# The long convolutions' filter on four quadrants of TensorE's array instead of two

## What is computed

```python
    h = jnp.sin(freq * (h @ w3 + b3))
    h = (h @ w_proj).reshape(L, HYENA_ORDER, N_DIRECTIONS, HYENA_WIDTH)
    ...
    decay = jnp.exp(-t * jnp.abs(deltas)[None, :])
    return h * decay[:, None, None, :]

def two_sided_spectrum(h):
    ...
    k_full = jnp.concatenate([k_fwd, jnp.zeros_like(k_fwd[:1]), k_bwd[:0:-1]], axis=0)
    return jnp.fft.rfft(k_full, n=2 * L, axis=0)

    for o in range(HYENA_ORDER):
        y = gates[o] * fft_conv(y, k_f[:, o], hyena_d[o])
```

## Time and profile before

| | |
|---|---|
| median of 3 runs | 4593.53 us |
| the profiled execution | 4597.2 us |
| its span (first to last instruction) | 4595.4 us |
| TensorE busy (PE) | 4273.0 us, 93% |
| VectorE busy (DVE) | 2845.9 us, 62% |
| ScalarE busy (ACT) | 1916.2 us, 42% |
| mean granted clock of TensorE | 0.967 of full speed |
| the jobs of the long convolutions | 2220 to 2690 us of the span |

### The profile page before, as it was taken

One profiled execution on the slowest core, in us unless ns is written; L12 is line 12 of the kernel. 1 busy time (PEld: TensorE's weight loads), 2 busy tenths in 40 slices (PEclk: granted clock), 3 DMA queues, 4 the chain that ended last, 5 costly groups with the idle time before them and its releaser, 6 DMA issues.

```text
span 4595.4 us, 62423 instructions
## 1 busy us (share of the span) xinstructions
PE 4273.0 (93%) x24340; PEld 3462.5 (75%) x24372; DVE 2845.9 (62%) x3887; ACT 1916.2 (42%) x3543; POOL 1126.8 (25%) x733
## 2 busy tenths in 40 slices
PE   7999999999899989999899979899999998988689
PEld 4888888889788777788677658677878777766467
DVE  5688888871666532045466667475675673577666
ACT  5111111111566631122566546454564562466453
POOL 2111111110333311011021112453554442233212
PEclk9999999999999999999999989999999999999799
DMA  4111111122544321111589852444434334443663
GB/s 169 51 51 51 51 51 51 55 68 90 190 131 132 120 99 48 55 65 66 203 273 292 281 215 90 124 136 127 142 115 129 118 123 126 124 118 108 193 194 133
DMA packets 606956, 569.59 MB, mean 124 GB/s; under 512 B 59772, under 2 KB 517312, under 8 KB 601674
## 3 DMA queue, kind: packets, MB, share of 16 engines
q1 hardware_dynamic: 557630, 482.52, 33.9%
q10 hardware_dynamic: 49036, 83.09, 4.9%
HBM read 385.61 MB, written 179.90 MB: 123 GB/s over the span
## 4 chain that ended last, share of the span: by engine, by line
PE 74%; DVE 10%; ACT 6%; issue 4%; DMA 4%; SPq 2%; POOL 1%; ACTq 0%; DVEq 0%; POOLq 0%
PE ps L227 10%; PE ps L226 10%; PE ps L228 10%; PE ps L252 3%; PE ps L251 3%; PE ps L253 3%; PE ps L3604 2%; PE ps L3605 2%; PE ps L3606 2%; DVE rec_x L3338 2%; PE ps L3725 2%; PE ps L2488 1%; PE ps L2487 1%; PE ps L2489 1%; PE ps L239 1%
## 5 line engine op out<-in xcount | busy, mean ns | idle before, releaser
L226 PE MATMUL ps<-hh,wsplit 128*128 128x512 f32 x2048 | 819.2, 400 | 8.2 <-DVE hl L1376 4.3
L227 PE MATMUL ps<-hl,wsplit 128*128 128x512 f32 x2048 | 814.1, 397 | 0.0
L228 PE MATMUL ps<-hh,wsplit 128*128 128x512 f32 x2048 | 809.1, 395 | 0.0
L952 DVE SCALAR_TENSOR_TENSOR conv_acc<-conv_in,pcol,conv_acc 128x1024 f32<-128x1024 f32 x480 | 687.9, 1433 | 14.8
L218 POOL TENSOR_TENSOR wsplit<-wraw,wsplit 128x1024 fp32r<-128x1024 f32 x72 | 201.9, 2815 | 1347.1 <-ACT wsplit L213 1347.1
L2822 POOL TENSOR_TENSOR w<-w_raw,w 128x1024 fp32r<-128x1024 f32 x144 | 352.5, 2454 | 647.0 <-ACT w L2816 646.8
L226 PEld LDWEIGHTS ps<-hh,wsplit 128*128 128x128 f32 x2048 | 387.3, 189 | 108.9 <-issue 7.4
L227 PEld LDWEIGHTS ps<-hl,wsplit 128*128 128x128 f32 x2048 | 390.3, 191 | 93.4 <-issue 4.3
L228 PEld LDWEIGHTS ps<-hh,wsplit 128*128 128x128 f32 x2048 | 386.2, 189 | 88.3
L3604 PE MATMUL ps<-h_hi,w 128*128 128x512 f32 x896 | 376.6, 420 | 4.4 <-DVE h_lo L3392 4.4
L3605 PE MATMUL ps<-h_lo,w 128*128 128x512 f32 x896 | 358.7, 400 | 0.0
(11 more groups left out here) (389 smaller groups left out, 9249.3 us busy)
## 6 DMA issues: line engine op xcount, KB each, us to landing
w_raw<-in_w_in SPq DMA_DIRECT2D x144, 512.0 KB, 4.2
wraw<-in_w_in SPq DMA_DIRECT2D x72, 512.0 KB, 3.9
sh<-hy_ak ACTq DMA_DIRECT2D x48, 512.0 KB, 3.8
g_tiles<-b_ost SPq DMA_DIRECT2D x80, 256.0 KB, 3.5
wo_raw<-in_w_out SPq DMA_DIRECT2D x32, 512.0 KB, 5.6
sh<-hy_ad ACTq DMA_DIRECT2D x32, 512.0 KB, 9.5
hy_kt<-sh SPq DMA_DIRECT2D x32, 512.0 KB, 7.1
hy_dd<-sh SPq DMA_DIRECT2D x32, 512.0 KB, 6.7
```

The lines of the kernel that those rows point to most:

```text
L226: e.matmul(p[:, :], wh, c.HH[tb][:, k, :], start=k == 0, stop=False)
L227: e.matmul(p[:, :], wh, c.HL[tb][:, k, :], start=False, stop=False)
L228: t = e.matmul(p[:, :], wl, c.HH[tb][:, k, :], start=False, stop=k == 7)
L952: e.scalar_tensor_tensor(v, a[:, h * 1024 + j:(h + 1) * 1024 + j], c.convw(j, ch), v, ALU.mult, ALU.add) \
```

## The change

`hy_filter` takes two banks at a time, for groups g and g + 1. The even group is made as before. For the odd group the halves are written crosswise: the forward half of `G` goes to the bank's partitions 64 to 127, the backward one to 0 to 63. So four matmuls in a row use the four quadrants. There is one signal for a pair instead of one for a group, and VectorE's product of an odd group waits for the same signal as that of the even one. What stands crosswise is put right by data: the times of the decay are exchanged for the odd groups, and wk uses for them a second matrix, `WK[1]`, which is `WK` with its rows rolled by 64. The constant k_wk is 256 columns wide now, and it takes one more DMA of 64 KB. Some constants lie elsewhere in SBUF.

```diff
-    k["k_wk"] = wk
+    k["k_wk"] = np.concatenate([wk, np.roll(wk, 64, axis=0)], 1)
...
-    k["k_time"] = -np.concatenate([ends[tf.T], ends[tb.T]], 0)
+    times = np.concatenate([ends[tf.T], ends[tb.T]], 0).reshape(128, 4, 2, 4)
+    times[:, :, 1] = np.roll(times[:, :, 1], 64, axis=0)
+    k["k_time"] = -times.reshape(128, 32)
...
+    L.WK = [view("hy_wk", at_wk, 128), view("hy_wk_turned", al(128), 128)]
...
-        for n, (dst, src) in enumerate([(L.WK, A["k_wk"]), (flat(L.WA), A["k_wa"]), (flat(L.WAI), A["k_wai"]), (L.rate, A["k_rate"]), (L.time, A["k_time"])]):
+        for n, (dst, src) in enumerate([(L.WK[0], A["k_wk"][:, 0:128]), (L.WK[1], A["k_wk"][:, 128:256]), (flat(L.WA), A["k_wa"]), (flat(L.WAI), A["k_wai"]), (L.rate, A["k_rate"]), (L.time, A["k_time"])]):
...
-                e.wait_ge(*L.pe["kg", i, g])
+                e.wait_ge(*L.pe["kg", i, g - g % 2])
...
-    for g in range(8):
-        p = take_bank(e, c, ("kg", i, g))
+    for g in range(0, 8, 2):
+        p = [take_bank(e, c, ("kg", i, g + r)) for r in range(2)]
         for j in range(4):
-            for h in range(2):
-                rr = slice(64 * h, 64 * h + 64)
-                t = e.matmul(p[rr, j * 128:(j + 1) * 128], L.G[rr, 4 * g + j, :], L.WP[rr, od, cs], start=True, stop=True)
+            for r in range(2):
+                for h in range(2):
+                    rr, to = slice(64 * h, 64 * h + 64), slice(64 * (h ^ r), 64 * (h ^ r) + 64)
+                    t = e.matmul(p[r][to, j * 128:(j + 1) * 128], L.G[rr, 4 * (g + r) + j, :], L.WP[rr, od, cs], start=True, stop=True)
         t.then_inc(*L.pe.up(("kg", i, g)))
...
-                e.matmul(p[:, :], L.WK, flat(L.KT[:, 4 * g:4 * g + 4, :]), start=True, stop=True).then_inc(*L.pe.up(("wk", i, g)))
+                e.matmul(p[:, :], L.WK[g % 2], flat(L.KT[:, 4 * g:4 * g + 4, :]), start=True, stop=True).then_inc(*L.pe.up(("wk", i, g)))
```

More of the change, by code:

```diff
@@ L1786, in hy_layout @@
     L.rate = view("hy_rate", c.base, 512)
-    L.WK, L.WA, L.WAI = view("hy_wk", al(128), 128), view("hy_wa", al(256), 2, 128), view("hy_wai", al(256), 2, 128)
+    at_wk = al(128)
+    L.WA, L.WAI = view("hy_wa", al(256), 2, 128), view("hy_wai", al(256), 2, 128)
     L.dr, L.time = view("hy_d", al(256), 2, 128), view("hy_time", al(32), 32)
+    L.WK = [view("hy_wk", at_wk, 128), view("hy_wk_turned", al(128), 128)]
     L.DEC += [view(f"hy_dec{2 + q}", al(512), 512) for q in range(2)] + high
```

## The result

The changed kernel took 4604.72 us (median of 13 runs, 4597.2 to 4612.39) against 4593.97 us for the kernel before, in 13 runs between them: a ratio of 1.0025, 95% interval 1.0017 to 1.0033. It is slower, by 10.8 us. The forecast said +4.6 us, and 4604.7 lies above the end of its range, 4604.0.

What follows compares the result with a forecast made beforehand. VectorE's chain, ending within 0.17 us of TensorE's filter, was taken to hold wk. Gains of 0.4 and 1.0 us and 6 us of clock falls gave +4.6 us, forecast 4598.0 us, range 4592.0 to 4604.0.

Steps and rivals of the forecast that it cites:

- Who waits for whom: In front of wk: VectorE's add of the row of D lets wk go, while TensorE's filter ends within 0.17 us of it.
- Rival D: Filter: the work saved is the time saved, 29 us, giving 4565; chance 0.02.
- Rival C: Filter: four quadrants don't run side by side, a pair still takes 1.84 us, giving 4593.5; chance 0.13.
- The clock falls: Granted clock drops after TensorE's idle time before wk, in 5 of jobs 1 to 7 at 1.2 us each: +6 us.
- the wait for the shuffle: Job 0, behind wk: the kernel waits for the shuffle by DMA anyway, so 0.1 us at most, counted as nothing.
- Jobs 2 to 7, forecast -0.4: wk starts at 2329.05 instead of 2329.12 in job 2: 0.07 us earlier per job, 0.4 us for six.
- Job 1, forecast -1.0: Job 1's filter starts late after slow ks; wk started at 2278.77 though the add ended at 2277.69, giving 1.0 us.
- The likeliest case: Whole kernel: falls in some jobs, 4594.5 to 4602, likeliest 4598.0; chance 0.50.
- rival B: wk of jobs 1 to 7: the clock falls in every job, nearly whole in wk, 1.7 us each, giving 4604; chance 0.20.
- 0.22 for "slower": Whole kernel: chance 0.22 of being slower by over 0.2%, above 4602.7 us.

Runs made afterwards that it cites:

- the fill: The change with the third pair's filter matmuls made three times in jobs 1 to 7; 4588.5 us against 4596.53 before (0.9982), later 0.9985 and 0.999.
- a slower filter with less idle time: The change with each pair's even group made wholly before the odd one, two quadrants at a time; 4598.49 us against 4596.53 before (1.0006).
- the kernel with zeros: The kernel before with three of four filter columns per group written as zeros by one bf16 matmul; 4596.69 us against 4596.53 (1.0005).
- the filter made twice: The change with every filter matmul done twice into the same place; 4606.35 us against 4596.53 before (1.0022).

## Why the prediction was wrong

**Who waits for whom: right.** VectorE lets wk go, as the earlier trace rows said. The bursts and the pauses came where they were worked out (0.55, 1.78 and 0.77 us, forecast 0.7, 1.95 and 0.9), and 18.9 us less of busy TensorE time bought nothing. Rival D is out. Rival C is out too: 27 ns a record, not 56.

**The clock falls: right in kind, number and price.** "A fall in 5 of the 7 jobs from 1 to 7, at 1.2 us each" is what three of four profiles show, at 6.4 / 5 = 1.3 us each in the first; the fourth has two. That it is the idle time that brings them was shown: filling it takes them away (the fill, in all its profiles, with no pause over 1.3 us left in front of wk), a slower filter with less idle time (1.29 us at the longest) has none in jobs 1 to 7, and the kernel with zeros gets them without any crossed quadrant, behind pauses of 1.55 us. The sixth fall, in job 0, costs 0.4 us at its wk (which starts 10.1 us behind the filter's start, before 9.7), and the next filter starts 51.3 us behind it where before it was 50.8 and 51.9: the wait for the shuffle covers it, as forecast. In jobs 2 to 7 of the change each filter has one pause of 1.8 us, and the falls came at its end or within 2.5 us of it. Its length alone doesn't decide: jobs without a fall have it too, and in the filter made twice a stop of 1.58 us brought none.

**What failed is the sum around the falls**, "-0.4 - 1.0 + 6 = +4.6 us", and the range built on it: its two gains, 1.4 us together, came to 0.5, and it has no term for anything outside jobs 1 to 7. The measured terms:

- Jobs 2 to 7, forecast -0.4: wk starts 0.02 us earlier in each, -0.1 in all. The step behind it was that wk starts 0.10 us behind VectorE, as after a product. Behind the add it starts 0.15 us late now, and 0.16 before: at 2329.12 the add had been holding wk nearly as long as the filter did.
- Job 1, forecast -1.0: from the start of its filter to that of wk it is 6.16 us now and was 7.13, so this gain did come; wk starts 0.15 us behind the add, for 1.08 us before. But from the start of filter 1 to that of filter 2 it is 49.8 us now and was 50.2, only 0.4 us less. The other 0.6 us are lost behind wk, in job 0's binv and the da behind it. The low stretch at 2301.5 reaches into da here; in the second profile of the change it lies under bursts that wait anyway, and there filter 2 starts 48.2 us behind filter 1. The last burst of binv and da, in the first profile and then in the second:

```profile
2301.50 2.04 PE L2186 MATMUL ps<-hy_dd,hy_wi 128*128 128x128 f32 x8 [1.03 <-POOL hy_dd L2114]
2303.34 7.83 PE L2168 MATMUL ps<-hy_u,hy_wa 128*128 128x512 f32 x16
```

```profile
2301.81 1.13 PE L2186 MATMUL ps<-hy_dd,hy_wi 128*128 128x128 f32 x8 [0.27 <-POOL hy_dd L2114]
2302.78 7.04 PE L2168 MATMUL ps<-hy_u,hy_wa 128*128 128x512 f32 x16
```

- The falls, forecast +6: +6.4.

That makes +5.9 us. Adding it up in time gives the same: from filter 1 to filter 7 the three profiles with five falls take 311.9 us and both of before 307.6, +4.3, and job 7's fall adds 1.7 us behind that. The whole stage is longer by more, 478.7 us in the mean for 470.8. The rest, 1.9 us, lies behind filter 7, where the last db waits for a transfer. Its rows in the two profiles of before and in the first of the change:

```profile
2637.89 9.51 PE L2171 MATMUL ps<-hy_dd,hy_wx 128*128 128x128 f32 x64 [7.14 <-DMA hy_dd<-sh]
```

```profile
2640.30 9.01 PE L2171 MATMUL ps<-hy_dd,hy_wx 128*128 128x128 f32 x64 [8.26 <-DMA hy_dd<-sh]
```

```profile
2642.32 9.26 PE L2176 MATMUL ps<-hy_dd,hy_wx 128*128 128x128 f32 x64 [8.70 <-DMA hy_dd<-sh]
```

Before alone differs by 1.1 us in this wait, and by 2.8 us in the whole stretch from filter 7 to the end of the stage (110.5 and 113.3), so no part of it is put down to the change.

Of the 8.6 us that three measurements give in the mean, 5.9 are thus placed for an execution with five falls, and 2.7 are not; each measurement's own interval is some 8 us wide. The fourth profile, with two falls, has a stage of 471.6 us, 0.8 us longer than before, so over all executions the placed part can be less. In the mean of its four profiles the change has a third block 2.8 us longer than the two of before have, with 5.0 us more at a granted clock of 0.50, which would be as much as is missing. But before alone differs by 2.5 us there, and the part in front of job 0's filter, whose arithmetic is the same in all these kernels, ends anywhere from 2216.4 to 2223.1 us, so this is not shown. The prediction had put all of this at nothing.

The first of the three measurements happened to lie 2 us above their mean. The likeliest case was too low by the 0.9 us of gains that didn't come or were lost again, and by the unplaced part. The range was wrong for a plainer reason: the far end of rival B had been worked out as 4605, measured noise was not added to it, and the range was closed at 4604.0. With 6 us from the clock, 0.22 for "slower" counted on every small gain coming in full. That the measured 4604.7 stands beside rival B's 4604 is chance: B wanted a fall in every job, nearly whole in wk, and no profile has that.

**What stays open.** The fill gains 8.0, 9.4 and 7.3 us against before in its three measurements, but its stage is no shorter (471.9 us in the mean, for 470.8). Its profiles have the difference in the third block, whose code is untouched: 1669.4 us in the mean, where before and change lie between 1673.9 and 1682.7. The clock goes with it: at 0.50 that block spends 159.4 us in the mean behind the fill, 175.3 before and 180.3 in the change. At 0.42 us each the 15.9 us less make 6.7 of the 8.5 us by which the block is shorter than before. Why the clock falls less there behind a filled filter no run shows, and one execution of the fill differs from another by up to 43 us in it. So the fill's gain over before is measured and its place is known, but its cause is open; that it takes away the falls in front of wk is shown.

## What to carry to other kernels

Before speeding up the busiest engine, find the wait that ends last at the next step: where another engine arrives within some tenths of a microsecond (0.17 us here), the work saved becomes idle time. On TensorE that idle time was not free here: behind pauses of 1.8 us the clock stood at 0.50, and wk lost 6.4 us in seven jobs. So read the granted clock behind pauses of similar length in the same trace, and put the price into the sum. Where the other engine's chain can't be shortened enough, harmless repeated matmuls in the pause can be worth more than the work they cost: a chain 0.75 us shorter and one pair made twice gave 4586 us, where the change alone gave 4602 to 4606; about half of the gain over before lies in the stage itself. More repeats are not always better: with three of them TensorE stood still in two jobs, for 0.40 and 1.00 us, with nothing to wait for that the profile shows, and wk started 0.5 and 0.9 us later there than with two.

## What the runs showed of the hardware

Matmuls of 64 x 64 on four quadrants, both directions crossed, follow each other at 27 ns a record, on two quadrants at 56 ns, in the mixed order at 41 ns. At the short pitch TensorE stood still after 156 records for 1.11 us, and in the filled hole after 92 for 0.40 us, with nothing to wait for that the profile shows, and it went on 1.3 to 1.6 us after a packet on the queue of instructions had landed. The falls are not independent draws: in three of four executions of the change they came in the same jobs, with the lengths of wk within 0.06 us of each other. And what a low stretch costs depends on what lies under it: 1.7 us where all of its 3.4 us lie in wk, none to be seen under bursts that wait for another engine anyway (in job 0's binv of the second profile they still start 2.15 to 2.17 us apart), and over the whole third block 0.42 us for each microsecond.
